# The FFN's down projection as seven half products in three slices, modulation rows made in the mixers, and Silu on ScalarE

## The chip, the cores and the metric

The kernel runs on one NeuronCore of a Trainium2 chip. The metric is the device time of one execution, in microseconds; lower is better. TensorE's time on a matmul is given by the profile in records: one fp32 matmul of the program leaves two MATMUL records and two LDWEIGHTS records, so 16 matmuls are 32 records.

## The reference, cut to what matters

Two blocks follow each other over 256 tokens of width 1024. The first has two layers. Each is `x + post_norm(mixer(pre_norm(x)))` and then `x + post_norm(swiglu(pre_norm(x)))`. Layer 0's mixer is a conformer convolution (31 taps) beside a gated linear recurrence, layer 1's an mLSTM. The feed-forward part, with 2816 hidden columns, is

```
def _swiglu(xn, w_gate, w_up, w_down):
    g = jnp.einsum('bsd,df->bsf', xn, w_gate)
    up = jnp.einsum('bsd,df->bsf', xn, w_up)
    return jnp.einsum('bsf,fd->bsd', jax.nn.silu(g) * up, w_down)
```

The second block (attention with spatial gating, a short convolution, and two mixtures of 32 experts) takes its shifts, scales and gates from "modulations": `silu(c) @ w_ada[l] + b_ada[l]` for both of its layers, 6144 columns each, and the first 2048 columns of layer 0 for `c_ctx` too. They depend on no token, so the kernel makes them during the first block, when DMA and VectorE have room.

## The kernel before, in words

Everything is fp32 and transposed: activations lie as tiles of 128 features (partitions) by 256 tokens. `h` is the FFN's input (8 tiles), `ff` its hidden activation (22 tiles), `u` and `sq` are other 8-tile buffers (`h`, `u`, `sq` and `ff` print as hsq and work in the profile).

**The weight stream.** SyncE (SP) loads weights in a fixed order, `chunks`, each up to 2 MB (128 partitions by 8 x 512 values), into `ring`, 6 slots used in turn. `load(n)` first waits until chunk n-6 is released by its reader, so SP stands still there with all that is behind it in the order. All these transfers are in SP's one queue. The list is: 0 to 3 input weights of mixer 0, 4 the first output half, 5 a slot without a transfer (convolution taps), 6 the second output half, then FFN 0, the mLSTM's six input and two output chunks, FFN 1, and the second block. `spread_groups` (L1736, DMA issues at L1741) copies activations between partitions with 16 small transfers, once for the recurrence's convolution and once for the 31-tap one. The second time stands ahead of `load(6)`.

**Mixer 0.** TensorE multiplies chunks 0 to 3 (L656, L568), does small products of the recurrence (L695), and then, when the second spread has landed, the 31-tap convolution (L670, 256 records), then layer norm sums and the output projection (L713, L585, L727).

**FFN, gate and up.** Hidden columns are done in chunks c = 0 to 5 of 512 (the last 256). c = 0 is a seam (`seam_chunk`, L638): it starts on the first 128 tokens while the norm of the others is still made. c = 5 is done plainly (L568, 128x256). c = 1 to 4, `quarter_products` (L785), use the Strassen-Winograd scheme on 2x2 blocks (tokens halved, columns halved, features halved): seven products P1, P5, P6, P2, P7, P3, P4 in place of eight, each 16 matmuls of 128 columns for gate and up together. VectorE makes the sums of weights (L2400, L2408, L2417, L2427, 128x1024) and tokens (L2383); ScalarE copies partial results between PSUM banks ("seeded"), VectorE adds the product P5 into two banks (L2444). Then ScalarE takes a Sigmoid of the gates and VectorE does two multiplications, gate by sigmoid (L2431) and that by up (L2432), three times a chunk.

**FFN, down.** Two column halves (c = 0, 1), each with 22 tiles of `ff` as contraction and four output tiles: 176 matmuls of 256 columns a layer (L870). In layer 0 the last output tile is done in token halves (22 + 22 matmuls of 128 columns, L870 and L898), so that the norm of the first tokens can be made under the second half.

**Modulations.** VectorE makes a row of 512 modulation values from one chunk of `w_ada` as one L2368 and seven L2215 instructions (`ada_make`), in half rows set between the FFN's other steps (`ada_steps`): 28 rows, since four chunks serve two conditions. TensorE collects four rows at a time (`ada_group`, L595, 8 records) in bank 7, four groups in layer 0 and three in layer 1, and turns each layer's result once (`ada_turned`, L607).

**Constants.** Two transfers (`spare_front`, `spare_back`, L1757 and L1758) reload constants over the FFN's weight sums, once the last quarter product is done, ahead of the next chunks.

Of the kernel before, what the change touches and what calls it, by code (L numbers as in the profile page):

```python
# [69 lines left out]
QW = HTL * CH // 2  # L70
ADA_LOADS = ((), (0, 1), (2,), (3, 4), (5,), (6,))
ADA_IN_DOWN = 7
ADA_ORDER = ((4, 5, 6, 7, 8, 9, 10, 11, 0, 1, 2, 3), tuple(range(12)))
# [75 lines left out]
def build(nc, a, out):  # L149
    with ExitStack() as ctx:  # L150
# [107 lines left out]
        fifth = tmp[:].rearrange("p a t -> p (a t)")  # L258

# [112 lines left out]
        down_part = sem("down_part_done")  # L372
# [26 lines left out]
        chunk(None)  # L399
        chunk(a["ab_w_out"][1])  # L400

        gate_chunks, up_chunks, down_chunks, ada_chunks = ([[], []] for i in range(4))

        def ffn_chunks(l):

            def ada_chunk(i):
                ada_chunks[l].append(len(chunks))
                chunk(a["w_ada"][l, ADA_ORDER[l][i]])

# [8 lines left out]
            for c in range(2):  # L418
                for k0 in range(0, FT, KT):
                    nk = min(KT, FT - k0)  # L420
                    down_chunks[l].append(len(chunks))
                    chunk(a["w_ff_down"][l, c, :, k0:k0 + nk, :], nk=nk)
                    if len(ada_chunks[l]) < 12:
                        ada_chunk(len(ada_chunks[l]))

        ffn_chunks(0)
        ffn_last = len(chunks) - 1
        for c in (0, 1, 2, 3, 4, 5):
            chunk(a["ml_w_in"][c])
        for c in range(2):  # L430
            chunk(a["ml_w_out"][c])
# [20 lines left out]
        seam_rows = (HTL + 2 * HTL, KT - 1 + 2, KT - 3 + 2 * 3)  # L452
        final_squares = 6 * KT + sum(seam_rows)
# [36 lines left out]
        def conditions(l, i):  # L490

            return 2 if l == 0 and i >= 8 else 1

        ADA_GROUPS = (4, 3)
        ADA_COPIES = (3, 1)
# [15 lines left out]
        def _(pe):  # L511
# [3 lines left out]
            made_so_far = [0]  # L515
# [24 lines left out]
            def next_chunk(n=None):  # L540
                if n is None:
                    n = state["chunk"]
# [45 lines left out]
            def ada_group(l, i):  # L588

                turn.take(S["ada_made"], GROUPS)  # L590
                if i == 0:
                    open_bank(7)
                last_group = i == ADA_GROUPS[l] - 1
                for g in range(GROUPS):
                    last = mm(ps[QUAD * g:QUAD * g + QUAD, 7, :], one_hot(i, QUAD), made[:, (GROUPS * i + g) % MADE, :],  # L595
                              start=(i == 0), stop=last_group, skip_group_check=True)
                if last_group:
                    close_bank(7, last, tiles_act, S["ada_rows"])
                else:
                    turn.give(last, S["ada_summed"])  # L600

            def ada_turned(l):
# [5 lines left out]
                close_bank(b, last, tiles_act, S["ada_raw"], reads=ADA_COPIES[l])  # L608
# [18 lines left out]
            def seam_chunk(n, w):  # L627

                banks = [next_bank() for m in range(4)]
                for t in range(TT):  # L630
                    for k in range(KT):
                        if k == 2:
# [83 lines left out]
            def halves_project():  # L716

                (first, w_0), (second, w_1) = next_chunk(), next_chunk(TAPS_SLOT + 1)
# [50 lines left out]
            def quarter_products(l, c):  # L769

                n = 4 * l + c - FAST.start
# [5 lines left out]
                def add(b, tile_of, rows, begins, first_sum=None):  # L777

                    for w in range(2):
                        if first_sum is not None:  # L780
                            pe.wait_ge(S["weights_summed"], 8 * n + first_sum + w)
# [32 lines left out]
                pe.wait_ge(S["tokens_summed"], 4 * l + 4)  # L814
                add(6, summed(0), sum_tokens[:, 0], True, 1)
                pe.wait_ge(S["seeded"], 4 * n + 1)
                add(1, summed(1), sum_tokens[:, 1], False, 5)
                add(0, plain(HTL, 0), high[:, :, half(0)], False)
                pe.wait_ge(S["seeded"], 4 * n + 3)
                pe.wait_ge(S["weights_summed"], 8 * n + 4)  # L820
                add(2, plain(0, 2), sum_tokens[:, 2], False)
                add(1, summed(2), high[:, :, half(1)], False, 7)
                pe.wait_ge(S["seeded"], 4 * n + 4)
# [2311 lines left out]
```

## Time and profile before

| | |
|---|---|
| median of three runs | 1881.2 us (1881.18 to 1881.66) |
| the profiled execution | 1880.99 us, its span 1879.2 us |
| TensorE busy | 1821.9 us, 97% |
| VectorE busy | 657.0 us, 35% |
| ScalarE busy | 376.0 us, 20% |
| mean DMA rate | 317 GB/s |
| FFN 0: c = 1 to 4, c = 5, down | 147 to 249, 249 to 263, 263 to 343 us |
| FFN 1: c = 1 to 4, c = 5, down | 516 to 622, 622 to 636, 636 to 715 us |
| the two stages of experts | about 860 to 1300 and 1460 to 1879 us |

In a line of the timeline the first number is the start, the second the time until the group's end, and "x64" how many records it joins; what stands in brackets is the engine's idle time before it and what ended that. Times on ScalarE and VectorE are ends of single instructions; matmuls overlap, so that 64 records of 380 ns take 13.8 us together. An instruction waits for the last of what it needs, and a full TensorE says only that it had work, not that the work was short.

### The profile page before, as it was taken

Reading aid. Unit: us, or ns where it says so; the run is one execution under the profiler, and the core shown is the slowest. Engines: PE = TensorE matmul, PEld = TensorE weight load, DVE = VectorE, ACT = ScalarE, POOL = GpSimd, SP = SyncE. Lnnn points to the kernel's source line nnn. Section 1 sums busy time; section 2 is a strip of 40 time slices with the busy share of each in tenths; the row PEclk is TensorE's granted clock in tenths of the full one; section 3 lists DMA queues with packets and bytes.
Section 4 is the critical chain, followed back from the end, with each engine's and each line's share of the span. In section 5 each row is a group of like instructions: output and inputs, shape, how many; then the busy total and the mean of one; then the engine's idle time right before and its main releaser. Section 6 shows DMA issues by size and latency. Waiting matters only on the chain.

```text
span 1879.2 us, 24366 instructions
## 1 busy us (share of the span) xinstructions
PE 1821.9 (97%) x10194; PEld 1200.2 (64%) x10196; DVE 657.0 (35%) x1353; ACT 376.0 (20%) x831; POOL 15.4 (1%) x31
## 2 busy tenths in 40 slices
PE   8999999999999999999999998999999999998998
PEld 7799988857999888575444433335885444433333
DVE  3278876432678653533111110112233111110112
ACT  3441110322311103423211110112013211111111
POOL 1000000000000100000000000000000000000000
PEclk9999999999999999999999999999999999999999
DMA  9744686732356883349999999999568999999996
GB/s 301 241 179 171 272 336 286 293 121 90 135 234 258 336 327 141 129 177 343 427 426 423 434 429 432 434 425 425 225 235 308 420 427 423 432 433 430 432 427 265
DMA packets 54323, 595.81 MB, mean 317 GB/s; under 512 B 6096, under 2 KB 20688, under 8 KB 24656
## 3 DMA queue, kind: packets, MB, share of 16 engines
q1 hardware_dynamic: 53648, 592.29, 76.9%
q10 hardware_dynamic: 576, 2.10, 0.3%
q8 instruction: 75, 1.23, 0.3%
q14 instruction: 24, 0.20, 0.0%
HBM read 588.90 MB, written 1.05 MB: 314 GB/s over the span
## 4 chain that ended last, share of the span: by engine, by line
PE 77%; DMA 19%; DVE 3%; ACT 1%; issue 0%; SPq 0%; DVEq 0%; ACTq 0%
PE ps L1357 18%; DMA ring<-in_w_up 17%; PE ps L568 16%; PE ps L870 8%; PE ps L785 7%; PE ps L1487 7%; PE ps L1312 3%; DMA ring<-in_w_ff_up 2%; PE ps L1305 2%; PE ps L638 2%; PE ps L924 1%; PE ps L727 1%; PE ps L656 1%; PE ps L670 1%; PE ps L1126 1%; PE ps L1086 1%
## 5 line engine op out<-in xcount | busy, mean ns | idle before, releaser
L1357 PE MATMUL ps<-ring,work 128*64 128x512 f32 x1792 | 405.8, 607 | 34.9 <-DMA ring<-in_w_up 29.6
L1357 PEld LDWEIGHTS ps<-ring,work 128*64 128x64 f32 x1792 | 128.8, 140 | 300.3 <-issue 248.2
L1804 ACT ACTIVATE work<-ps 128x512 f32<-128x512 f32 (+1 forms) x167 | 87.9, 532 | 696.2 <-PE ps L1487 248.7
L568 PE MATMUL ps<-hsq,ring 128*128 128x256 f32 x1024 | 225.1, 381 | 0.8 <-DVE hsq L2270 0.8
L568 PEld LDWEIGHTS ps<-hsq,ring 128*128 128x128 f32 x1024 | 193.9, 190 | 28.6 <-issue 2.8
L1487 PE MATMUL ps<-ring,work 128*64 128x512 f32 x864 | 191.6, 596 | 0.3
L2847 DVE TENSOR_TENSOR work<-ps,work 128x512 f32<-128x512 f32 x26 | 18.0, 691 | 389.2 <-ACT work L1804 389.2
L870 PE MATMUL ps<-work,ring 128*128 128x256 f32 (+1 forms) x704 | 149.5, 374 | 0.0
L2215 DVE SCALAR_TENSOR_TENSOR work<-ring,silu_c,work 128x512 f32<-128x512 f32 x196 | 143.7, 754 | 4.8
L870 PEld LDWEIGHTS ps<-work,ring 128*128 128x128 f32 x704 | 130.3, 190 | 20.7 <-issue 4.2
L1487 PEld LDWEIGHTS ps<-ring,work 128*64 128x64 f32 x864 | 59.6, 137 | 115.7 <-issue 113.9
L1312 PE MATMUL ps<-work 128*128 128x256 f32 x512 | 121.5, 382 | 0.0
L785 PE MATMUL ps<-hsq,ring 128*128 128x128 f32 x1024 | 118.1, 276 | 0.5 <-DVE work L2432 0.3
L785 PEld LDWEIGHTS ps<-hsq,ring 128*128 128x128 f32 x1024 | 116.2, 192 | 2.5 <-issue 2.2
L1312 PEld LDWEIGHTS ps<-work 128*128 128x128 f32 x512 | 92.7, 191 | 18.0 <-issue 8.1
L785 PE MATMUL ps<-hsq,spare 128*128 128x128 f32 x768 | 90.5, 279 | 2.0 <-ACT ps L1804 1.9
L785 PEld LDWEIGHTS ps<-hsq,spare 128*128 128x128 f32 x768 | 89.0, 195 | 2.7 <-ACT ps L1804 2.4
L2850 DVE TENSOR_TENSOR work<-ps,work 128x512 f32<-128x512 f32 x26 | 18.0, 691 | 195.0 <-PE ps L1357 195.0
L1804 ACT ACTIVATE work<-hsq 128x512 f32 x60 | 38.0, 634 | 209.8 <-PE ps L1357 202.5
L568 PE MATMUL ps<-work,ring 128*128 128x256 f32 x352 | 79.1, 382 | 0.4 <-DVE work L2687 0.4
L568 PEld LDWEIGHTS ps<-work,ring 128*128 128x128 f32 x352 | 66.2, 190 | 12.8 <-issue 3.5
L1357 PE MATMUL ps<-spare,work 128*64 128x512 f32 x192 | 56.2, 593 | 0.0
(347 smaller groups left out, 1617.9 us busy)
## 6 DMA issues: line engine op xcount, KB each, us to landing
ring<-in_w_up SPq DMA_DIRECT2D x16, 4096.0 KB, 22.0
ring<-in_w_down SPq DMA_DIRECT2D x16, 4096.0 KB, 20.4
ring<-in_w_gate SPq DMA_DIRECT2D x16, 4096.0 KB, 21.4
ring<-in_w_ada SPq DMA_DIRECT2D x24, 2048.0 KB, 11.1
ring<-in_w_gate SPq DMA_DIRECT2D x24, 2048.0 KB, 11.5
ring<-in_w_up SPq DMA_DIRECT2D x22, 2048.0 KB, 14.4
ring<-in_w_down SPq DMA_DIRECT2D x20, 2048.0 KB, 14.8
ring<-in_w_ff_gate SPq DMA_DIRECT2D x10, 2048.0 KB, 13.1
```

Of the source, the lines that this page charges most:

```text
L568: last = mm(ps[:, b, 0:T], w[:, k, m * P:(m + 1) * P], rhs[:, k, :], start=(i == 0), stop=(i == nk - 1))
L638: last = mm(ps[:, banks[m], half(t)], w[:, k, m * P:(m + 1) * P], u[:, k, half(t)], start=(k == 0), stop=(k == KT - 1))
L656: last = mm(ps[:, banks[m], 0:T], w[:, k, m * P:(m + 1) * P], u[:, k, :], start=(k == 0), stop=(k == KT - 1))
L670: last = mm(ps[QUAD * g:QUAD * g + QUAD, b, 0:T], taps_of(GROUPS * j + g), data_of(GROUPS * j + g), start=start, stop=stop)
L785: last = mm(ps[:, b, at:at + P], tile_of(w, k, m), rows[:, k, :], start=(begins and w == m == k == 0), stop=(k == HTL - 1), skip_group_che ...
L870: last = mm(ps[:, banks[m], 0:cols.stop], w[:, k - k0, m * P:(m + 1) * P], ff[:, k, cols], start=(k == 0), stop=(k == FT - 1))
L1305: last = mm(ps[:, 3 - half, k * PAIR:(k + 1) * PAIR], htok[:, t, (4 * half + k) * P:(4 * half + k + 1) * P], pick[:, t, :], start=(t == 0) ...
L1312: return mm(ps[:, 4 + m // 2, (m % 2) * T:(m % 2 + 1) * T], rows, first_spread if of_first else spread, start=begins and m % 2 == 0, stop= ...
L1357: last = mm(ps[e * CAP:(e + 1) * CAP, w, :], xg[:, k, e * CAP:(e + 1) * CAP], tile_of(first, w, i, 2 * k // KT, e, k % HTL), start=(k == 0 ...
L1487: last = mm(to, hg[:, at:at + CAP], tile, start=(k == 0), stop=(k == HTL - 1))
L1804: return nc.scalar.activation(out_, in_, f, bias=bias, scale=scale, **kw)
L2215: return V.scalar_tensor_tensor(out=out_, in0=in0, scalar=scalar, in1=in1, op0=op0, op1=op1)
```

## The change

1. **Down in seven products.** The 22 tiles of `ff` are split into tiles 0 to 10 and 11 to 21, the two operands of the 2x2 scheme's contraction; tokens and output columns are halved. The 11 tile pairs are taken in three slices of 4, 4 and 3 (`down_slice`). A slice has two chunks of weights (one for each column half) and seven products of 4 output tiles by 4 (or 3) contraction tiles, 128 columns each: 28 x 11 = 308 matmuls a layer. VectorE makes the sums of tokens (`down_tokens`, four a slice, 128x512) and of weights (`down_plus`, `down_second`, `down_less`, `down_fourth`, eight a slice, 128x1024) for each slice. The seven products add up in seven banks over the three slices. In the last slice VectorE joins the banks (`join_down`: four joins, three sums of 128x512) between the products, and one more matmul, identity by four tiles of `h`, adds the last term (P3's bank). ScalarE squares and copies four tiles at a time (`down_rows`) and VectorE sums four squares with one reduction (`sum_of_rows`). The norm of the first tokens starts under P5; `seam_chunk` after FFN 0 takes the other norm's sum two steps later (`late=4`).
2. **Modulation rows in the mixers.** Layer 0's first four `w_ada` chunks, which serve two conditions, become "pair" chunks: two loaded in mixer 0 (chunks 6 and 8, the second output half between them is 7), two in mixer 1 (after its second and fourth input chunk). VectorE makes their eight rows there in eight pieces of 8 instructions (`pair_part`; two pieces a chunk). The second `spread_groups` now stands behind `load(8)`. The other rows are 11 in FFN 0 (three of them of layer 1) and 9 in FFN 1. TensorE collects them in four groups a layer, the first of pair rows right after the seam, and FFN 1 has one more `ada_turned`.
3. **Gate function on ScalarE.** In c = 1 to 4 Silu replaces Sigmoid, and the multiplication L2431 goes: 24 instructions.
4. **Around it.** The constants' transfers wait for the last product of down, behind five chunks of the next stage; the waits for them on TensorE and VectorE move later. The context's squares go to other buffers, ahead of the sigmoids of c = 5.

```
@@ chunks
+        pair_chunk(PAIRS[0][0])
+        second_out = len(chunks)
         chunk(a["ab_w_out"][1])
+        pair_chunk(PAIRS[0][1])
+        ab_last = len(chunks) - 1
...
+            for s, n in enumerate(DOWN_SLICES):
+                two = {}
+                for c in (1, 0):
+                    two[c] = len(chunks)
+                    chunk(a["w_ff_down"][l, s, c, :, 0:2 * n, :], nk=2 * n)
+                down_chunks[l].append((two[0], two[1]))
+                for i in ADA_IN_DOWN[l][s]:
+                    ada_chunk(i)
@@ SP's order
-                if n == TAPS_SLOT + 1:
+                if n == ab_last + 1:
                     sp.wait_ge(S["lru_conv"], HTL)
                     spread_groups(rep_glu, cpad, REP, S["glu"], taps_spread)
...
+                load(n)
                 for l in range(2):
-                    if n == max(down_chunks[l]) + 1:
-                        sp.wait_ge(S["quarter_product"], 4 * QUARTERS * (l + 1))
+                    if n == max(down_chunks[l][-1]) + 6:
+                        sp.wait_ge(S["quarter_product"], UNITS * QUARTERS * (l + 1))
@@ TensorE, slices 0 and 1
+                    sums_by(4, 2)
+                    add("P6", summed(1), tokens[1])
+                    sums_by(6, 3)
+                    add("P7", plain(wb, 0), tokens[2])
+                    add("P5", summed(0), tokens[0])
+                    pe.wait_ge(S["tokens_summed"], tokens_by(l, s) + 4)
+                    add("P4", plain(wb, nk), tokens[3])
+                    release(nb, S["quarter_product"])
+                    add("P1", plain(wa, 0), low[:, :, half(0)])
+                    add("P2", plain(wa, nk), high[:, :, half(0)])
+                    pe.wait_ge(S["weights_summed"], 8 * u + 8)
+                    add("P3", summed(2), high[:, :, half(1)])
@@ TensorE, last slice: P1, P6, group, P7, (joined 1) P2, turned, (joined 2) P4, (3) P5, (4) P3
+                pe.wait_ge(S["proj_copied"], freed[S["proj_copied"]])
+                turn.give(mm(ps[:, DOWN_BANKS["P3"], :].rearrange("p (m t) -> p m t", m=4), ident, h[:, 4:KT, half(1)], start=False,
+                             stop=True, skip_group_check=True), S["quarter_product"])
@@ VectorE, mixers
+            pair_part(0, 0, 0)
+            pair_part(0, 0, 1)
             turn.take(S["lru_conv"], HTL)
             turn.take(S["lru_gate"], 2 * HTL)
             step(V.tensor_tensor(bx[:], bx[:], xr[:], ALU.mult))
+            pair_part(0, 1, 0)
...
                 step(V.tensor_tensor(cv[:, j, :], cv[:, j, :], tmp[:, 0, :], ALU.subtract), S["ln_ready"])
+            pair_part(0, 1, 1)
@@ VectorE, the gate in c = 1 to 4
-                step(V.tensor_tensor(sig, gates_, sig, ALU.mult))
-                step(V.tensor_tensor(rows, ups, sig, ALU.mult), S["quarter_read"])
+                step(V.tensor_tensor(rows, ups, silu, ALU.mult), S["quarter_read"])
@@ VectorE, down
                 last_quarter(n, c)
+                down_tokens(l, 0)
                 ada_steps(1)
+                down_plus(l, 0)
                 hidden(FAST.stop * HTL)
+                down_second(l, 0)
+                down_less(l, 0)
+                hidden(FAST.stop * HTL + 1)
                 ada_steps(1)
+                down_fourth(l, 0)
+                ada_steps(2)
+                down_tokens(l, 1)
...
```

## Rows read from the trace of the kernel before

**Rows 1.** The page, sections 1 and 2: busy time, and GB/s in 40 slices of 47 us.

```profile
PE 1821.9 (97%) x10194; PEld 1200.2 (64%) x10196; DVE 657.0 (35%) x1353; ACT 376.0 (20%) x831; POOL 15.4 (1%) x31
...
GB/s 301 241 179 171 272 336 286 293 121 90 135 234 258 336 327 141 129 177 343 427 426 423 434 429 432 434 425 425 225 235 308 420 427 423 432 433 430 432 427 265
```

**Rows 2.** What TensorE waited for: line and releaser, us in total, times, longest.

```profile
PE ps L1357 <- DMA ring<-in_w_up: 29.6, 15, 2.6
...
PE ps L785 <- ACT ps L1804: 1.9, 1, 1.9
```

**Rows 3.** Chain of waits, pieces: start us, us, line and records (128 columns L785, 256 L870).

```profile
151.06 21.45 PE ps L785 x192
...
223.89 25.21 PE ps L785 x224
...
635.91 13.81 PE ps L870 x64
```

**Rows 4.** Timeline, TensorE: down of FFN 0, and the seam after it.

```profile
262.75 13.98 PE L870 MATMUL ps<-work,ring 128*128 128x256 f32 x64
...
276.66 1.06 PE L595 MATMUL ps<-work,hot 128*32 128x512 f32 x8
...
343.30 1.95 PE L638 MATMUL ps<-work,ring 128*128 128x128 f32 x16
```

**Rows 5.** Timeline, TensorE: down of FFN 1 from its start to the next product.

```profile
635.74 1.46 PE L870 MATMUL ps<-work,ring 128*128 128x256 f32 x6
...
714.97 1.24 PE L568 MATMUL ps<-work,ring 128*128 128x256 f32 x5
```

**Rows 6.** Timeline of mixer 1: 16 records of 512 columns (for the identity matmul).

```profile
373.68 7.13 PE L924 MATMUL ps<-ring,hsq 128*128 128x512 f32 x16
```

**Rows 7.** VectorE by line and shape: xcount | busy us, mean ns | idle before.

```profile
L2400 DVE TENSOR_TENSOR spare<-ring 128x1024 f32<-128x1024 f32 x16 | 19.1, 1222 | 13.6 <-DMA ring<-in_w_ff_up 8.8 <-DMA ring<-in_w_ff_gate 4.7
...
L2383 DVE TENSOR_TENSOR hsq<-hsq 128x512 f32<-128x512 f32 x8 | 5.5, 691 | 0.3
...
L2645 DVE TENSOR_REDUCE small<-work 128x1 f32<-128x512 f32 x2 | 1.4, 686 | 2.4 <-ACT work L1804 2.3
```

**Rows 8.** Timeline, FFN 0: load at the end of c = 4, half rows in down.

```profile
249.13 0.33 SPq L1603 DMA_DIRECT2D ring<-in_w_ff_down  x1
...
282.23 9.36 DVE L2215 SCALAR_TENSOR_TENSOR work<-ring,silu_c,work 128x512 f32<-128x512 f32 x14
```

**Rows 9.** Timeline, FFN 1, c = 2 and 3, around TensorE's wait, and the clock of that window.

```profile
541.50 0.33 SPq L1603 DMA_DIRECT2D ring<-in_w_ada  x1
...
562.40 1.22 DVE L2400 TENSOR_TENSOR spare<-ring 128x1024 f32<-128x1024 f32 x1 [3.67 <-DMA ring<-in_w_ff_up]
...
573.98 0.69 DVE L2431 TENSOR_TENSOR work<-ps,work 128x512 f32<-128x512 f32 x1 [0.73 <-ACT work L1804]
...
576.13 5.47 PE L785 MATMUL ps<-hsq,spare 128*128 128x128 f32 x32 [1.91 <-ACT ps L1804]
...
575.00:580.00 5.00, 3.87 (x21) 3.88 (x22) 4.83 (x8) 1.08 (x2) 0.00 (x0) 0.69 0.99 423
```

**Rows 10.** Timeline, mixer 0: spreads and loads on SP, and where TensorE needs the second spread.

```profile
37.97 0.59 SPq L1603 DMA_DIRECT2D ring<-in_ab_w_out  x1
...
52.89 10.34 SPq L1741 DMA_DIRECT2D work<-work  x16
...
69.71 5.60 PE L670 MATMUL ps<-work,ring 128*32 128x256 f32 x100
```

**Rows 11.** DMA between 31 and 39 us, where spreads stood behind others: GB/s in 40 parts.

```profile
GB/s 184 287 128 205 143 149 230 246 169 174 184 246 190 184 200 184 190 266 190 195 189 179 215 236 205 200 230 220 200 205 215 210 210 195 195 205 179 220 200 205
```

**Rows 12.** VectorE's idle stretches in the mixers (in brackets), timeline.

```profile
66.97 1.23 DVE L2324 TENSOR_TENSOR work<-work 128x1024 f32<-128x1024 f32 x1 [15.90 <-ACT work L1804]
...
94.91 1.75 DVE L2219 RECIPROCAL rstd<-root 128x256 f32<-128x256 f32 x1 [6.87 <-ACT root L1804]
...
373.89 0.42 DVE L2550 COPY work<-ps 128x256 f32<-128x256 f32 x1 [11.66 <-PE ps L916]
```

More of the change, by code:

```diff
@@ L488, in build, with unit, slice_unit, product_done @@
         SPARE_DMAS = [sum(spare_dmas(i, half) for i, _ in matrices(RING // 2, TURNING - 1)) for half in range(2)]
[L490 to L495, printed above, removed]
+        ADA_COPIES = (4, 2)
+        PAIR_COPIES = 2
+        made_by = 0
+        for l in range(2):
+            for n in pair_chunks[2 * l:2 * l + 2]:
+                made_by += 2
+                released[n] = (S["ada_made"], made_by)
+            for n in ada_chunks[l]:
+                made_by += 1
+                released[n] = (S["ada_made"], made_by)
+        def unit(l, c):
+            return UNITS * l + c - FAST.start
+        def slice_unit(l, s):
+            return UNITS * l + len(FAST) + s
+        def product_done(u, name):
+            s = u % UNITS - len(FAST)
+            order = ORDERS["gate" if s < 0 else "last" if s == len(DOWN_SLICES) - 1 else "down"]
+            return QUARTERS * u + order.index(name) + 1
+        def seeds_before(l, c):
+            return (4 * len(FAST) + 1) * l + 4 * (c - FAST.start)
+        def joins_before(l, c):
+            return (len(FAST) + 4) * l + c - FAST.start
+        def tokens_by(l, s=-1):
+            return 4 * (len(DOWN_SLICES) + 1) * l + 4 * (s + 1)
         def masks_by(pair):
@@ L890, in ffn @@
-                state["chunk"] = max(down_chunks[l]) + 1
-                if l:
-                    return
-                open_bank(6)
-                for k in range(FT):
-                    if k == KT - 2:
-                        sum_stats(half(0))
-                    n, w = held[k // KT]
-                    last = mm(ps[:, 6, 0:P], w[:, k % KT, 3 * P:4 * P], ff[:, k, half(1)], start=(k == 0),
-                              stop=(k == FT - 1))
-                    if k % KT == KT - 1:
-                        turn.give(last, down_part)
-                        release(n, down_part)
@@ L2303, in _, with ada_part, pair_part, ada_make @@
             step(V.tensor_scalar(lamt[:, 16:20], lamt[:, 12:16], LRU_C / 2, None, ALU.mult), S["lam_ready"])
+            def ada_part(n, part, rows):
+                slot = ring[:, n % RING, :].rearrange("p (k c) -> p k c", k=KT)
+                if part == 0:
+                    dve.wait_ge(slot_loaded[n % RING], landed(n))
+                for k in range(part * KT // 2, (part + 1) * KT // 2):
+                    for w, to in enumerate(rows):
+                        by = silu_c[:, k, w:w + 1]
+                        if k:
+                            turn.own(vchain, len(rows) - 1 - (w if k == KT - 1 else 0))
+                            last = stt(to, slot[:, k, :], by, to, ALU.mult, ALU.add)
+                        else:
+                            last = V.tensor_scalar(to, slot[:, k, :], by, None, ALU.mult)
+                        turn.give(last, S["ada_made"] if k == KT - 1 else vchain)
+            def pair_part(l, i, part):
+                ada_part(pair_chunks[2 * l + i], part, pair_rows[2 * i:2 * i + 2])
+            def ada_make(l, q, part):
+                if part == 0 and q >= MADE and (q - MADE) % GROUPS == 0:
+                    turn.take(S["ada_summed"])
+                ada_part(ada_chunks[l][q], part, [made[:, q % MADE, :]])
             def make_taps(dst, w):
@@ new lines, in down_second @@
+            def down_second(l, s):
+                n, u = down_chunks[l][s][0], slice_unit(l, s)
+                dve.wait_ge(slot_loaded[n % RING], landed(n))
+                dve.wait_ge(S["quarter_product"], product_done(u - 1, "P6"))
+                for w in range(2):
+                    dve.wait_ge(S["weights_summed"], 8 * u + 1 + w)
+                    ((w11, _), _), sums = down_blocks(l, s, w)
+                    turn.give(V.tensor_tensor(sums[1], sums[0], w11, ALU.subtract), S["weights_summed"])
@@ L2515, in ffn @@
                         weights_fourth(l, c)
+                    elif l:
+                        turn.take(S["ada_raw"], PAIR_COPIES)
                     ada_steps(2)
```

501 lines of the change are left out of this document (330 added, 171 removed).

## The prediction

> **What bounds the kernel now.** I read the page first [rows 1]: TensorE is busy 97% of the span. Two stages differ in kind. From slice 19 of 40 on, with a break in the middle, DMA runs at 420 to 434 GB/s and TensorE's waits name expert weights [rows 2]; before that DMA moves 90 to 343 GB/s a slice, and TensorE hardly waits. The whole change lies in the first 16 slices, where TensorE's work is the time. What is won there moves the start of everything behind it, the loads of the experts too, since they wait for slots released by the stage before. So I sum TensorE's path through mixers and FFNs, and then look for waits that the change brings.
>
> The price of a record comes from the chain's long pieces [rows 3]: 128 columns take 21.45/192 = 0.1117 and 25.21/224 = 0.1125 us, 256 columns 13.81/64 = 0.2158. I take 0.1122.
>
> **Down, seven for eight.** FFN 0 before: 262.75 to 343.30, 80.55 us [rows 4]. Its parts: 308 wide records (66.5), 88 narrow (9.9), three groups of modulation rows at 276.66 to 277.65, so 1.0 each, and 1.1 of small things (the turn, a norm's sum, gaps). After: 616 narrow records, 69.1; the identity matmul, two records of 512 columns at 7.13/16 = 0.44 [rows 6], 0.9; two groups, 2.0; the same small things, 1.0. That is 73.0, so -7.6. FFN 1 before: 714.97 - 635.74 = 79.23 [rows 5], all 352 records wide. After: 73.1, so -6.1. The bounds of the rate move the two by -0.6 and +0.4 together.
>
> The row on this has a rule beside it that speaks against narrow products. The Trainium skill (TensorE: Matmul & The Clock Gate, section LDWEIGHTS) has a weight load cost its columns over 1.2, 107 ns for 128, however few columns the matmul then streams: going from 256 to 128 columns leaves no room behind the load. By that rule alone 616 loads would take 65.9 us where the row's price gives 69.1, so the load would just keep up; the row decides.
>
> **Modulation groups.** Each FFN has a pair group after the seam, +1.0 each, and FFN 1 one more turn, +0.4: +2.4. TensorE's work alone is then -7.6 - 6.1 + 2.4 = -11.3.
>
> **Can VectorE feed it?** 128x1024 sums are 1.22 us, 128x512 ones 0.69 [rows 7], a half row 9.36/14 x 4 = 2.7 [rows 8]. In FFN 0 between 249.6 and slice 2's start: tokens 3 x 4 x 0.7 = 8, weights 24 x about 1.1 = 26, ten half rows 27, hidden tiles 2: 63 us of about 65. I walked it in order: slice 0 starts at 262.8 and a product takes 32 x 0.1122 = 3.6, so slice 1 starts at 289 and its first sums are done at 283; slice 2 starts at 314, P6 needs its sums at 317, they are done at 310. The joins: P7 ends at 323, two additions of 0.7, P4 starts after P2 and the turn at 326. Each is covered by a product in front. FFN 1 has 10 us more (context norm) and fewer rows; slack 6 at slice 1. Cost 0, by the 6 us of slack; without it see the third case.
>
> **Start of down.** Slice 0 needs both its chunks where down needed one. Their slots come free when c = 4 ends (the load at 249.13 [rows 8]). Two times 2.1 MB at 430 GB/s is 9.8 us: 259.3 at the soonest. In rows 9 three loads and a 1 MB one (7.3 MB, 17.1 us by rate) issued from 541.5 were there at 562.4, 3.8 us more; so 259.3 to 263.1. `down_second` adds 2.4 after that, and TensorE is there at 262.7: a wait of 0 to 2.9 a layer. I take 0.35 each, near the low end since only two chunks are in the queue: +0.7.
>
> **Silu.** VectorE loses 24 multiplications, off the path in FFN 0. In FFN 1 they are on it: the load at 562.4 sets off sums, two gate steps, ScalarE's copy, and TensorE waits 1.9 us until 576.13 [rows 9]. Its next 32 records take 5.47 where the piece before took 3.6 to 3.7, and the granted clock of 575 to 580 is 0.69: part at 1.2 GHz after that idle time, 1.7 us lost. Leaving out 0.42 and 0.69, plus issue gaps, gives -1.2, and a wait of about 1.1 stays. Bounds: 0, and -2.9 if after the shorter wait the clock stays at 2.4 GHz. I take -1.2. ScalarE's table loads for Silu fall where it idles for products.
>
> **Ends of down.** FFN 0: the first tokens' norm starts under P5, about 3.7 us ahead of the seam, before 2.9; the second norm's sum is taken two steps later and is ready. Cost 0; 0 to 1. FFN 1: after P3 a 128x512 square and a 128x512 reduction (0.69 [rows 7]) and an addition stand where a 128x256 square and addition stood; the sum then comes 0.3 later than TensorE's place for it: +0.4, 0 to 0.8. The constants now come after two output chunks: 4.2 + 2.7 MB from 6.5 us before down's end, there at about 12 us after it, needed at 16. Cost 0.
>
> **Mixers, VectorE.** A `pair_part` is 8 instructions, 5.4 us. In mixer 0 two go into the 15.9 us of idle before 66.97, one into the 9.4 behind, one into the 6.9 before 94.91; in mixer 1 two (10.8) into the 11.7 before 373.89 [rows 12], the others between heads. The tightest has 0.9 to spare. Cost 0.
>
> **Mixer 0, the queue.** Here is what the change costs. SP's order was: load 4 at 37.97, then wait for the recurrence's convolution and issue the 16 spreads from 52.89 to 62.6, TensorE needing them at 69.71 [rows 10]. Now loads 6, 7 and 8 are ahead of the spreads: 6 and 7 right after 4 (their slots are long free), 8 when chunk 2 is released, at about 50.4. Spreads move slowly: with a backlog (31 to 39 us) DMA gives 180 to 230 GB/s, mostly near 205 [rows 11]. Chunk 4 ended near 47.3. Then 6 and 7: +9.8, 57.1; 8: +4.9, 62.0; 16 spreads of 142 KB, 2.27 MB at 205: +11.1, 73.1, and 0.4 for the last to land: 73.5 against 69.7. TensorE waits 3.8. After it the clock: the only row with such a wait lost 1.7 [rows 9], so +5.5 in all. Bounds: 0 if the spreads are not held back, 8.4 with 184 GB/s (+1.2) and twice the clock's loss.
>
> The Trainium skill (DMA: Bandwidth & Descriptors, Queues, rings and completion order) says that each DMA engine consumes a queue's descriptors in ring order. By that rule the spreads stand behind all three loads and the 5.5 holds; without it the sum is the second case's.
>
> **Sum.** -11.3 - 1.2 + 0.7 + 0.4 + 5.5 = -5.9. The profiled execution took 1880.99, 1.8 more than its span; the median of the runs is 0.2 above it. From 1881.2: 1875.3.
>
> **The cases.**
> 1. *As summed*, 1875.3, by its own bounds 1872 to 1878.5. Chance 0.5.
> 2. *The spreads are in time* (the loads of pair chunks share the engines with them, or the rate in a mixed queue is higher): -5.5 more, 1869.8; 1866.5 to 1872. For it: in the middle of 37 to 47 us, loads and spreads went together. Against: that stretch was as long as the two one after the other. Chance 0.26.
> 3. *VectorE or the loads hold down back at the slice borders.* VectorE has 63 us of work in 65, and each chunk's slot waits for the product or row that uses it. Once it is over 6 us late, each layer's slices 1 and 2 wait for sums; with 3 us a layer and its clock loss the result is 1881 (1878 to 1885). For it: rows 9 show one late load running through to TensorE. Against: my walk. Chance 0.16.
> 4. *Slower: the narrow products in down are slower than in gate and up.* The place is both downs, where TensorE reads `ff`, sums and ring while VectorE writes sums and DMA fills slots at over 400 GB/s. 1232 records: it decides from 9.7/1232 = 7.9 ns a record more, 0.120 us; at 0.122 the result is 1887. Against it stands 0.1125 over 224 records under the same kinds of load [rows 3]. Chance 0.08.
>
> **Numbers.** No change to a measurement of this kernel is within 0.2%, 1877.4 to 1885.0. Faster: 0.44 of case 1, case 2, a little of 3: 0.71. Within: 0.06 of case 1 and most of 3: 0.2. Slower: 0.09. The range must hold 8 in 10: 1867 to 1880 holds cases 1 and 2 and the lower part of 3.
>
> **What the profile after would show.** Down as 616 records a layer in about 69 us and next to no wait in front of its products; 8 groups and 3 turns; no L2431; the context's squares ahead of FFN 1's down. In mixer 0 SP issues three loads between the two spreads, and the 31-tap convolution starts near 73.5 with a wait of 3 to 5 us on DMA and a lower clock right behind it; from there to the FFN everything is later by 5. In FFN 1 the wait in c = 3 is near 1.1. The experts' part keeps its length. I am wrong if the convolution starts before 71 (then case 2), if down's waits sum to over 4 us (case 3), or if 32 of its records take over 3.8 us (case 4).

## The result, and the profile after

The changed kernel takes 1892.64 us, median of five runs (1888.59 to 1894.71), against 1881.66 before: a ratio of 1.0057, 95% interval 1.0044 to 1.0070. It is slower by 0.57%. The forecast was 1875.3 with a range of 1867 to 1880, and the chance of slower was given as 0.09, for a cause (slow narrow records) that did not occur. The profiled execution took 1894.71, its span 1892.8 against 1879.2.

The page's first section, and what TensorE waited for in the changed kernel (line and releaser, us in total, times, longest):

```profile
PE 1813.4 (96%) x10688; PEld 1202.6 (64%) x10688; DVE 725.7 (38%) x1412; ACT 382.2 (20%) x824; POOL 17.4 (1%) x31
```

```profile
PE ps L1469 <- DMA ring<-in_w_up: 30.5, 16, 2.6
PE ps L734 <- issue: 14.7, 1, 14.7
...
PE ps L1469 <- issue: 4.5, 1, 4.5
...
PE ps L920 <- DVE spare L2659: 3.1, 2, 1.8
```

TensorE is busy 8.5 us less than in [rows 1], so the seven products for eight do save work, and the span is 13.6 us longer. The waits for expert weights are as in [rows 2] (L1357 is now L1469). New are one wait of 14.7 us at the 31-tap convolution (L734, before L670), two in front of down (L920), and 4.5 us inside the experts' second stage.

I set the starts of the same stages beside each other in both traces. What each stretch added to the lead of the old kernel, in us:

| stretch | added |
|---|---|
| start of the 31-tap convolution (69.71, now 84.31) | +14.6 |
| convolution to FFN 0's seam (half clock) | +2.05 |
| seams and pair groups, both FFNs | +1.8 |
| c = 1 to 4: FFN 0, FFN 1 | -0.4, -2.8 |
| c = 5 and the start of down, both | +3.9 |
| down FFN 0; down FFN 1 with all up to the experts | -7.3, -5.5 |
| seam behind FFN 0 | +1.1 |
| experts, first stage and the mixer behind | +0.1 |
| experts, second stage | +5.9 |
| sum | +13.5 |

Everything outside mixer 0 and the experts' second stage adds up to -9.1. The two others cost 22.6. The start of down in FFN 0 and the seam behind it, 73.24 us apart in the changed kernel, read:

```profile
281.65 3.81 PE L920 MATMUL ps<-hsq,spare 128*128 128x128 f32 x32 [1.78 <-DVE spare L2659]
...
354.89 3.73 PE L702 MATMUL ps<-work,ring 128*128 128x128 f32 x32
```

**Mixer 0.** The timeline of the changed kernel, TensorE and then SP's issues (start, time until the group's end), and what the spreads' line shows over both times 16 transfers (min/median/max, in ns and then in us):

```profile
84.31 16.07 PE L734 MATMUL ps<-work,ring 128*32 128x256 f32 x256 [14.65 <-issue]
```

```profile
50.36 0.33 SPq L1715 DMA_DIRECT2D ring<-in_w_ada  x1
52.76 19.29 SPq L1853 DMA_DIRECT2D work<-work  x16
72.09 1.17 SPq L1715 DMA_DIRECT2D ring<-in_w_ff_gate  x1
```

```profile
L1853 SPq DMA_DIRECT2D work<-work x32: 601/608/7774, 26.6 to 71.4; - x32
...
DMA to landing us min/median/max: 6.9/8.0/15.4
```

In [rows 10] the 16 issues took 10.34 us; now they take 19.29, for one of them, the ninth, took 7.77 (58.73 to 66.5). The first went out at 52.76 and landed at 67.0; the last went out at 71.4 and landed 12.8 us later, at 84.2; TensorE starts at 84.31. The profile calls the wait "issue", for it finds no releaser, but time and place name the spreads. The rate between 30 and 100 us, in 40 parts of 1.75 us, shows the loads at over 400 GB/s until 63 and the spreads near 200 behind them:

```profile
GB/s 320 112 164 200 211 206 225 209 235 422 431 403 431 412 431 412 440 449 409 209 122 163 206 207 207 205 225 191 200 377 361 161 53 20 0 0 0 9 0 0
```

The next windows give busy time, granted clock, DMA share and rate of two stretches:

```profile
64.00:78.00 14.00, 5.66 (x27) 4.63 (x25) 10.78 (x17) 9.54 (x16) 0.00 (x0) 0.89 1.08 189
78.00:84.00 6.00, 0.00 (x0) 0.00 (x0) 5.51 (x7) 1.65 (x2) 0.00 (x0) 0.50 0.95 288
```

From 64 to 84 us DMA moved 14 x 189 + 6 x 288 = 4.4 MB, and the 16 spreads are 2.27 MB. The rest is weights: the end of chunk 8, for which VectorE waited until 72.15, and FFN 0's first gate chunk, issued behind the spreads and under way with the last of them. TensorE's granted clock is 0.50 before it resumes, and the 256 records of the convolution then take 16.07 us where they took 14.02 before: the 2.05 us of the table.

**The experts' second stage.** The product of the second up matrix in the changed kernel:

```profile
1441.39 0.64 PE L1469 MATMUL ps<-ring,work 128*64 128x512 f32 x1
1446.51 8.78 PE L1469 MATMUL ps<-ring,work 128*64 128x512 f32 x31 [4.48 <-issue]
```

In the kernel before the same 32 records stand in one piece of 7.09 us from 1433.76 on. A matmul leaves two records, so this gap falls inside one. The profile names no releaser, and the program (`product_of`) has no wait at this place: it waits only ahead of the first and of the ninth matmul of this product.

### The profile page after: what moved, and what is told of

Same layout as the page of the kernel before. It is cut to its first block, busy times and chain, and to the rows that moved or that the text cites. A ratio compares the mean times of both kernels' runs of the same rounds, so it can differ in the third digit from the quotient of the medians.

```text
span 1892.8 us, 25468 instructions
## 1 busy us (share of the span) xinstructions
PE 1813.4 (96%) x10688; PEld 1202.6 (64%) x10688; DVE 725.7 (38%) x1412; ACT 382.2 (20%) x824; POOL 17.4 (1%) x31
## 4 chain that ended last, share of the span: by engine, by line
PE 75%; DMA 18%; DVE 4%; issue 2%; ACT 1%; SPq 0%; DVEq 0%; ACTq 0%
PE ps L1469 18%; DMA ring<-in_w_up 17%; PE ps L627 14%; PE ps L850 9%; PE ps L920 7%; PE ps L1599 7%; PE ps L1424 3%; PE ps L1417 2%; PE ps L1036 1%; PE ps L702 1%; PE ps L791 1%; DMA ring<-in_w_ff_up 1%; PE ps L734 1%; PE ps L720 1%; PE ps L1238 1%
## 5 line engine op out<-in xcount | busy, mean ns | idle before, releaser
L1469 PE MATMUL ps<-ring,work 128*64 128x512 f32 x1792 | 407.7, 608 | 39.2 <-DMA ring<-in_w_up 30.5
L1469 PEld LDWEIGHTS ps<-ring,work 128*64 128x64 f32 x1792 | 129.2, 140 | 306.0 <-issue 254.5
L2371 DVE SCALAR_TENSOR_TENSOR work<-ring,silu_c,work 128x512 f32<-128x512 f32 x140 | 105.9, 756 | 4.8
L627 PEld LDWEIGHTS ps<-work,ring 128*128 128x128 f32 x352 | 66.1, 190 | 13.8 <-issue 3.9
L1469 PE MATMUL ps<-spare,work 128*64 128x512 f32 x192 | 56.2, 592 | 0.0
L1916 ACT ACT_TABLE_LOAD x39 | 50.0, 1283 | 20.9 <-PE ps L1469 11.1
L702 PE MATMUL ps<-work,ring 128*128 128x128 f32 x384 | 45.6, 276 | 1.5 <-ACT work L1916 1.5
## 6 DMA issues: line engine op xcount, KB each, us to landing
ring<-in_w_gate SPq DMA_DIRECT2D x24, 2048.0 KB, 11.1
ring<-in_w_down SPq DMA_DIRECT2D x20, 2048.0 KB, 14.7
```

The lines of the kernel that those rows point to most:

```text
L627: last = mm(ps[:, b, 0:T], w[:, k, m * P:(m + 1) * P], rhs[:, k, :], start=(i == 0), stop=(i == nk - 1))
L702: last = mm(ps[:, banks[m], half(t)], w[:, k, m * P:(m + 1) * P], u[:, k, half(t)], start=(k == 0), stop=(k == KT - 1))
L1469: last = mm(ps[e * CAP:(e + 1) * CAP, w, :], xg[:, k, e * CAP:(e + 1) * CAP], tile_of(first, w, i, 2 * k // KT, e, k % HTL), start=(k == 0 ...
L1916: return nc.scalar.activation(out_, in_, f, bias=bias, scale=scale, **kw)
L2371: return V.scalar_tensor_tensor(out=out_, in0=in0, scalar=scalar, in1=in1, op0=op0, op1=op1)
```

## The experiments

Each is compared with the kernel before, timed anew beside it (medians of 1882.25 us for experiments 1 to 4, 1882.67 for 5 to 8, 1882.4 for 9 to 11). Each profile shows one execution. Three groups: the queue in mixer 0, the gap in the second stage, and the parts that behaved.

**1. One load ahead of the second spread.**

```
-                if n == ab_last + 1:
+                if n == TAPS_SLOT + 2:
                     sp.wait_ge(S["lru_conv"], HTL)
```

> The changed kernel with one edit: in SP's order the second spread stands behind one weight load (the first pair chunk, 6) and no longer behind three (6, 7 and 8). In the changed kernel the 31-tap convolution started at 84.31 us after 14.65 us of idle TensorE. Theory S (the loads ahead of the spreads in the one queue make the wait): chunk 6 landed at 58.0 where three loads shared the way; with only chunk 4 and 6 ahead the engines are through with them near 55, the 16 spreads are issued from 52.8 and 2.27 MB at about 205 GB/s end near 66 to 68, before TensorE is there at 69.7. The convolution starts near 69.7 without a wait, everything behind it is 14.6 + 2.1 (the half clock after the idle time) = 16.7 us earlier: 1892.6 - 16.7 = 1875.9 us, 1874 to 1880 with the spread of the runs. Chunk 8 would land near 73, as it did at 72.15. Rival (the second output half and the pair chunk, now late, stop VectorE's recurrence or the output projection): the wait comes back ahead of the recurrence's mix or the projection, 1880 to 1888.

1885.64 us, ratio 1.0019 (1.0009 to 1.0029). The convolution starts at 69.68, without a wait: the theory's step is right. But the rival is right too. Two lines of this kernel, VectorE's and TensorE's:

```profile
78.74 0.88 DVE L2501 TENSOR_SCALAR spare<-ring,silu_c 128x512 f32<-128x512 f32 x2 [10.24 <-DMA ring<-in_w_ada]
```

```profile
89.93 9.48 PE L791 MATMUL ps<-work,ring 128*128 128x256 f32 x32 [4.31 <-issue]
```

VectorE stands 10.24 us for the second pair chunk, and the recurrence's scan and the layer norm's start, next in its program, with it; the projection waits 4.31. The seam comes at 123.3 (before 116.46, changed 133.1).

**2. Two loads ahead** (`TAPS_SLOT + 3`).

> The changed kernel with the second spread behind two loads (6 and 7; both can be issued at once, their slots are free) and ahead of chunk 8. Theory S with the forecast's own rates (each load 4.9 us of queue at 430 GB/s, then 11.1 us for the spreads): 4.9 us less backlog than in the changed kernel, so the convolution starts at about 84.3 - 4.9 = 79.4, minus 2 us for chunk 8 that no longer shares the way: 77 to 80, total 1884 to 1888. If instead the jump comes from SP itself (one of its 16 issues took 7.8 us with three loads under way, as if the queue were full), two loads leave the queue room, no issue takes over 2 us, and the spreads land by 66 to 70: convolution at 69.7, total about 1876.

1890.1 us (1.0045; 1.0029 to 1.0060), above the 1884 to 1888 that was expected. Convolution at 76.91 after 7.24 us, and no issue of SP was long (16 in 11.61 us, the longest 1.54). The spreads are late all the same; SP's long issue is not needed for a wait.

**3. Three loads ahead, in the kernel before.**

```
-                if n == TAPS_SLOT + 1:
+                if n == TAPS_SLOT + 4:
                     sp.wait_ge(S["lru_conv"], HTL)
...
-                if n == 8:
+                if n == TAPS_SLOT + 5:
                     sp.dma_start(rw[:], a["router_w"]).then_inc(consts_loaded, 16)
```

> The kernel before, with nothing changed but SP's order: the second spread (and the router's weights behind it) stands behind three loads of 2 MB, here the second output half and FFN 0's first gate and up chunks (chunks 6, 7 and 8 of its own list, the third of which waits for the release of input chunk 2, as in the changed kernel). No pair rows, no half products in down. Theory S: the 31-tap convolution starts near 84 us where it started at 69.71, at half clock for its first part, and the total is 1881.7 + 16.7 = 1898.4 us, 1895 to 1901. Rival (the wait needs the rest of the change, VectorE's pair rows ahead of the recurrence above all): the convolution starts before 76 and the total is 1881 to 1889.

1893.25 us (1.0070; 1.0054 to 1.0085): this one edit makes the kernel before as slow as the changed one. In its profile the wait is 6.84 us, convolution at 77.67: less than 14.65, and between the numbers of theory and rival. FFN 0's seam is 9.4 us later than before; most of the other 3.5 of the 13.0 by which the span grew lies in the experts' part, whose code this edit leaves alone. So mixer 0 accounts for 9.4 us here, not for 16.65 as in the changed kernel, and the likeness of the totals is no measure of it.

**4. One load, and P1 and P2 first in slice 0.**

```
+                        add("P1", plain(wa, 0), low[:, :, half(0)])
+                        add("P2", plain(wa, nk), high[:, :, half(0)])
                     sums_by(4, 2)
...
+                    if s:
                         add("P1", plain(wa, 0), low[:, :, half(0)])
                         add("P2", plain(wa, nk), high[:, :, half(0)])
```

> The first kernel of this set (one load ahead of the spread), and in each layer's down TensorE takes slice 0's products in the order P1, P2, P6, P7, P5, P4, P3 in place of P6, P7, P5, P4, P1, P2, P3. P1 and P2 need one chunk as loaded and no sums of weights. In the changed kernel down started with a wait of 1.78 us (FFN 0) and 1.35 us (FFN 1) on VectorE's second sum, behind a chunk that landed 12.8 us after its issue. Theory: the chunk itself is there before TensorE (278.9 against 279.9), so both waits go: 3.1 us less than the first kernel of this set, with up to 0.5 us of half clock on top. Rival (the chunk's slot is released two products later, the next loads are late, and the same wait stands in front of slice 1 or 2): within 1 us of the first kernel.

1887.13 us (1.0027): no gain, the rival is right. In front of down there is no wait in either layer, but 1.16 us (FFN 0) and 1.50 (FFN 1) stand in front of slice 1: by the stages 1.9 and 1.5 us were won at the start of down and 2.0 and 1.8 lost behind it. Here the convolution waited 2.17 us with one load ahead.

**5. Dead code ahead of the jump, changed kernel.** The experts' stages begin with a branch on how many tokens an expert has; the code for all tokens is skipped.

```
+                if first == moe_first[1]:
+                    for _ in range(12):
+                        mm(ps[:, 7, T:2 * T], zeros[:, 0:P], zeros[:], start=False, stop=False, skip_group_check=True)
```

> The changed kernel with 12 matmuls more in the branch of TensorE's program that is not taken (all tokens for every expert) ahead of the second experts' stage; nothing that runs is changed, only where the code behind the jump lies, 48 instructions further. In the changed kernel and in all three kernels made from it so far TensorE stood 3.2 to 4.5 us in that stage after the first record of a matmul, where no wait on a semaphore can stand, with half clock behind it; the stage took 431.1 to 432.1 us where it took 425.7 and 426.1 in the two kernels with the old code. Theory C (the jump's target lies just ahead of the end of a block of code, and the next block is fetched only after the jump; the fetches show as 16384-byte packets of the instruction queue, 256 instructions of 64 bytes): the target now lies at the start of the next block, the gap is gone, the stage takes 426, and the total is 1892.6 - 6 = 1886.6 us (1885 to 1888.5). Rival (the gap is a late load or DMA traffic of instructions as such, which the small shift doesn't touch): gap still there, 1891 to 1894.

The gap is gone, and the second stage (from the product behind the gathering of tokens to the last group of L1469) takes 425.8 us where it took 431.6. The total is 1889.38 (1883.29 to 1895.94), above the 1885 to 1888.5 expected; in the profiled run the wait in mixer 0 was 17.09 us.

**6. Dead code, kernel before** (the same lines, 58 in place of 12).

> The kernel before with 58 matmuls (232 instructions) more in the same branch that is not taken, ahead of its second experts' stage. Counted in the two programs, the changed kernel's code in front of that jump is 1007 instructions longer, which is 17 less than four blocks of 256, and so puts the target 17 instructions lower in its block; 232 more put the target of the kernel before 24 lower. Theory C: the same standstill appears in a kernel that has nothing of the change, 3 to 5 us within a few matmuls behind the jump, the stage takes 430 to 432.5 and the total is 1882.2 + 6 = 1888 us (1886 to 1889.5). Rival (not the position of the code): 1881.5 to 1883, no gap.

1887.62 us (1.0026; 1.0017 to 1.0035), the second stage 432.8 (425.7 in the kernel before). The gap stands where it was foretold, in a kernel that has nothing of the change:

```profile
1433.25 1.08 PE L1357 MATMUL ps<-ring,work 128*64 128x512 f32 x4
1438.61 8.50 PE L1357 MATMUL ps<-ring,work 128*64 128x512 f32 x28 [4.28 <-issue]
```

The windows 1436 to 1438 and 1438 to 1444 of this kernel show what follows: a granted clock of 0.60 and 0.56.

```profile
1436.00:1438.00 2.00, 0.00 (x0) 0.00 (x0) 1.88 (x8) 0.00 (x0) 0.00 (x0) 0.60 0.90 367
1438.00:1444.00 6.00, 5.39 (x16) 2.29 (x17) 0.00 (x0) 0.00 (x0) 0.00 (x0) 0.56 0.48 205
```

Two more readings of the traces bear on the cause. The DMA view has this row of the instruction queue (packets, MB, share) for 1444.0 to 1445.2 in the changed kernel, and the second for 1436.4 to 1437.5 in this one:

```profile
q8 instruction: 1, 0.02, 5.2%
...
q8 instruction: 1, 0.02, 5.4%
```

So one packet of 16 KB moves 1.2 to 1.5 us before TensorE goes on (1446.51 and 1438.61), and none does in the 5 us from 1438.5 and from 1431. And the place of the gap moves with the code: the jump stands ahead of the last four of the 32 records of the gate product, so the gap comes 7 records behind its target in the changed kernel (4, 2 and 1) and 10 in this one (4, 2 and 4). Three records and their weight loads are 6 instructions, where the two targets, 17 and 24 instructions lower, lie 7 apart.

**7. Mixer 0 put in order.** Experiment 1 with the 12 dead matmuls, and:

```
-            pair_part(0, 1, 0)
             turn.take(S["lru_powers"], HTL)
...
-            pair_part(0, 1, 1)
+            pair_part(0, 1, 0)
             inverse_root()
...
                 step(V.tensor_tensor(y_conf[:, j, :], cv[:, j, :], sgate[:, j, :], ALU.mult), S["mixed"])
+            pair_part(0, 1, 1)
```

> The kernel with one load ahead of the second spread, plus two edits. First, VectorE takes the third and fourth piece of the pair rows (the second pair chunk, which then landed at 78.7 us) after the layer norm's subtractions and after the gated product, in place of ahead of the recurrence's scan; there VectorE had stood 10.24 us for the chunk, and TensorE 4.31 us in front of the output projection. Second, the 12 dead matmuls of the run above. Theory: the projection starts without a wait, FFN 0's seam near 116.5 (it was 123.3), and the standstill in the experts' second stage is gone: 1885.6 - 6.8 - 6 = 1872.8 us, 1871 to 1875. Rival for the mixer (the fourth piece, now at about 102 to 107.5, holds back the sums of squares ahead of FFN 0's norm): seam at 118 to 120, 1875 to 1877.

1875.6 us, ratio 0.9965 (0.9951 to 0.9979), 0.6 above the range that was expected. Convolution at 69.70, seam at 116.45, to 0.01 us where they were before.

**8. And P1 alone first in slice 0.**

```
+                        add("P1", plain(wa, 0), low[:, :, half(0)])
                     sums_by(4, 2)
...
+                    if s:
                         add("P1", plain(wa, 0), low[:, :, half(0)])
```

> The kernel just described, and in slice 0 of each down the product P1 (one chunk as loaded, no sums) ahead of P6; the rest keeps its order. With P1 and P2 both ahead the wait of 1.8 and 1.4 us in front of down went, and one of 1.2 and 1.5 us came in front of slice 1, since P4, whose token sums VectorE overwrites for slice 1, ended 7.2 us later. With P1 alone ahead it ends 3.6 us later, and VectorE's sums for slice 1 are then due at about 663.9 against 666.8 in FFN 1: no wait at either place. Theory: 3.1 us less than the kernel just described, 1869.7 us. Rival (VectorE is full in this stretch, and what is taken from one wait comes back at the next): within 0.8 us of it.

1869.57 us (1868.67 to 1870.03), ratio 0.9932 (0.9919 to 0.9946). It beats both kernels. Its starts of down, FFN 0 and FFN 1, and slice 0 behind each:

```profile
263.95 3.73 PE L920 MATMUL ps<-work,ring 128*128 128x128 f32 x32
267.52 3.74 PE L920 MATMUL ps<-hsq,spare 128*128 128x128 f32 x32
...
629.78 3.73 PE L920 MATMUL ps<-work,ring 128*128 128x128 f32 x32
633.35 3.74 PE L920 MATMUL ps<-hsq,spare 128*128 128x128 f32 x32
```

No idle time stands in brackets. Its convolution started at 70.60, without a wait. By the stages this edit gave 1.7 and 1.5 us; the rest of the 6.0 between the two medians lies in the experts' part, which differs by such amounts between profiles. That the total came out at the 1869.7 foretold is therefore luck: the start was 2.8 us above the 1872.8 assumed, and the step 2.9 us larger.

**9. Silu alone, kernel before** (three `ACT.Sigmoid` to `ACT.Silu`, L2431 left out).

> The kernel before with the third part of the change alone: Silu on ScalarE in place of Sigmoid in c = 1 to 4, and the multiplication of the gate by its sigmoid (24 instructions on VectorE) left out. The forecast gave it -1.2 us, with a bound of -2.9 if TensorE's clock holds behind the shorter wait; in the changed kernel c = 1 to 4 of FFN 1 took 103.3 us where they took 106.1, and FFN 0's 101.7 where they took 102.0. If Silu is the cause: 103.3 to 103.8 in FFN 1, the wait in c = 3 at 1.1 to 1.2 us without half clock behind it, total 1882.5 - 3 = 1879.5 us. If the cause lies elsewhere (the moved modulation rows, the order of the loads): 105 to 106, total 1881.3 to 1882.5.

1878.8 us, ratio 0.9982 (0.9973 to 0.9992). FFN 1's c = 1 to 4 take 103.2 us, FFN 0's 101.7. The wait in c = 3 and the clock around it:

```profile
574.27 3.84 PE L785 MATMUL ps<-hsq,spare 128*128 128x128 f32 x32 [1.19 <-ACT ps L1804]
```

```profile
573.00:578.00 5.00, 3.81 (x34) 3.73 (x34) 4.86 (x7) 1.11 (x3) 0.00 (x0) 1.00 1.03 439
```

**10 and 11. What makes 14.65 out of 6.84?** Experiment 5 with all of VectorE's pair pieces behind the convolution; and experiment 5 with mixer 0's pair chunks read from the projection's weights (its modulations are then other numbers).

> The changed kernel with the 12 dead matmuls, and all four pieces of the pair rows on VectorE behind the 31-tap convolution (the first after the layer norm's subtractions, three after the gated product); SP's order is the changed kernel's, three loads ahead of the second spread. The wait in front of the convolution was 14.65 and 17.1 us with VectorE at the pieces from 58 us on, and only 6.8 us in the kernel before with three loads and an idle VectorE. If VectorE's reads and writes slow the spreads: a wait of 6 to 9 us. If they don't: 12 to 17 us as in the changed kernel. The pieces behind the gated product delay FFN 0's first norm by some 8 us in either case, so the wait in front of the convolution is what counts, not the total: about 1889 + 8 less the gain.

> The changed kernel with the 12 dead matmuls, and the two pair chunks of mixer 0 loaded from the output projection's weights in place of the modulation's (same shape and size; the pair rows are then other numbers): everything else, SP's three loads ahead of the spread too, as in the changed kernel. If the source of the modulation chunks makes the queue slower than the kernel before with three loads was (6.8 us of wait against 14.65 and 17.1): a wait of 6 to 9 us and a total near 1883. If not: 12 to 17 us, 1888 to 1891.

The waits were 9.92 and 8.90 us. The second lies where the source's theory has it, but the first, with the old source, is just as short and lies between the numbers of its own theory; neither cause is shown. The first took 1892.51 us; the total of the second (2864.7) says nothing, since with other modulations the router's numbers send the kernel down the branch for all tokens.

## Why the prediction was wrong

**The step that failed: "Mixer 0, the queue".** The sentence "2.27 MB at 205: +11.1, 73.1, and 0.4 for the last to land" took the spreads as a block that begins when the loads end and then has the queue alone. The first half held roughly: the rate fell from over 400 to about 200 GB/s at 63 (forecast 62.0), though the last of chunk 8 came only at 72. The second didn't. The spreads needed 21 us from there, not 11.1. Two things fall into that time: SP got eight of them out by 58.7 and the other seven behind the long one only after 66.5, and the last ones shared the engines with the load issued behind them. How much each of the two took, no run separates. So the wait was 14.65, not 3.8, and the loss to the clock 2.05, not 1.7: 16.65 against 5.5, outside the bounds of 0 to 8.4. The bounds varied the rate and the clock's loss and left the two other things at nothing.

The Trainium skill's rule that each DMA engine consumes a queue's descriptors in ring order (DMA: Bandwidth & Descriptors, Queues, rings and completion order) gave the right side against case 2. The traces agree in so far as no spread landed before 67 us. They also show that transfers of one queue don't land in the order of their issue: chunk 8, issued ahead of all the spreads, landed at 72.1, five us behind the first of them, and by the 4.4 MB weights issued behind the spreads moved before the last spread was complete.

That the backlog makes the wait is shown: it is 0, 2.2, 0 and 0 us with one load ahead (experiments 1, 4, 7, 8), 7.2 with two, and 6.8, 8.9, 9.9, 14.7 and 17.1 with three. A second load is dearer than the first, and a third may cost nothing or 10 us. What chooses within 6.8 to 17.1 is open. Experiment 5's ten runs spread over 12.7 us, experiment 1's ten over 8.2 and experiment 8's five over 1.4, so part of it may differ from run to run in one kernel, which one profile of each can't show; VectorE's rows and the source of the chunks were tried once each and not settled. SP's longest single issue goes along with it: 1.5 and 2.1 us at waits of 7.2 and 6.8, 4.0 and 3.9 at 8.9 and 9.9, 7.8 at 14.7, 10.7 at 17.1. Which of the two is the cause isn't shown.

**A term the forecast didn't have: where the code lies.** "The experts' part keeps its length" was wrong by 5.9 us. The instruction queue (packets, MB, share of 16 engines) has this row in the changed kernel:

```profile
q8 instruction: 79, 1.29, 0.3%
```

These are 16 KB each, and before there were 75; TensorE's code in front of the jump was 1007 instructions shorter, counted in the two programs. Moving the target of a jump that is always taken by 48 instructions took the gap away, and by 232 in the old kernel made it. The Trainium skill (Runtime: NRT & Kernel Launch, Instruction fetch mechanics) has a taken branch stop the sequential prefetch. The traces agree in that the gap stands behind a taken jump, and add that the cost depends on the target's place in its block: none in the kernel before, and in the changed kernel and experiment 6, where the gap comes 7 and 10 records behind the target, 4.5 and 4.3 us and then half clock, together 5.9 and 7.2 for the stage. That the code's position sets the gap is shown both ways. That the gap is the fetch of the next block is argued, from the packet of 16 KB shortly before its end and from the place that moves with the code; why this packet comes no sooner stays open.

**By the forecast's other terms.**
- Down FFN 0, forecast -7.6: 73.24 us against 73.0, so -7.3. Its 32 narrow records take 3.74 us less the overlap, 3.57 from start to start (experiment 8's rows show the same), 0.112 each. Case 4 is refuted, and the concern that a narrow matmul leaves no room for its weight load shows no cost here: 0.112 is half of the 0.2158 of 256 columns.
- Down FFN 1 to its end, -6.1 and +0.4: -6.7, +0.8 for the tail and +0.5 behind it, -5.5 in all.
- Modulation groups, +2.4: +1.8.
- Silu, -1.2: -2.8 in FFN 1 and -0.4 in FFN 0. The mechanism was right and the bound was the value. The wait fell to 1.18, as forecast, and the clock held: 1.00 (584 to 589 us) where [rows 9] have 0.69. Experiment 9 has it alone: -2.8 and -0.4 too.
- Start of down, +0.7: +3.9. I took "near the low end". In FFN 0 chunk one landed 7.2 us and two 12.8 us after the issue, in the bounds of 10.2 to 14; VectorE then needs 2.4. In FFN 1 the chunks were there, and VectorE was late: two of its four 128x512 sums took 1.10 and 1.22 us in place of 0.69, and the instructions behind them were slow too. GpSimd was at work on the context's norm at that very time; in FFN 0, where it was idle, all four took 0.69, with DMA at 401 GB/s there and 406 in FFN 1. Experiments 7 and 8 show the same 1.10 and 1.22 beside GpSimd. So GpSimd is the likely cause, though no run tries it alone. The wait is 1.78 and 1.35, and 0.15 to 0.6 more lie in the stretch.

```profile
634.86 0.69 DVE L2630 TENSOR_TENSOR hsq<-work,hsq 128x512 f32<-128x512 f32 x1
635.58 1.10 DVE L2630 TENSOR_TENSOR hsq<-work 128x512 f32<-128x512 f32 x1
...
635.00 1.14 POOL L1896 TENSOR_TENSOR tmp<-tmp,spare 128x256 f32<-128x256 f32 x1 [616.50 <-ACT spare L1916]
```

- VectorE at the slice borders, 0: right. Between slices no wait stands, until experiment 4 moved P4 and used up the slack.
- Ends of down, 0 in FFN 0: +1.1, the second half's norm is late by 0.85.
- VectorE's pieces in the mixers, 0: right for time, but they depended on chunk 8, and experiment 1 shows the price as soon as it is late.

Without the queue and the code the forecast's terms give -11.4 and the traces -9.1. Experiment 8, which removes both, and the waits of down, measures -13.1; in its profile 11.5 of that are there when the experts begin.

## What to carry to other kernels

Small transfers that TensorE waits for do not belong behind weight loads in one queue: one 2 MB load ahead cost 0 to 2 us here, two 7, three 7 to 17. When they are moved forward, look at who waits for the load that is now late, and reorder that engine too. And when a stage that nobody changed gets slower, look for a gap without a releaser behind a jump: dead code in front of the target tests it without changing what runs.

## What the hardware showed that was not expected

- One DMA issue on SP took 7.77 us where the others took 0.6, with three loads of 2 MB and eight spreads issued shortly before.
- 48 instructions that never run were worth 5.8 us in a stage of 430 us; 232 in another kernel cost 7.2.
- Behind a wait of 1.91 us TensorE's next 32 records took 5.47 us [rows 9]; behind waits of 1.18, 1.35 and 1.78 us they took 3.84, 3.81 and 3.81.
- Two 128x512 sums of VectorE took 1.10 and 1.22 us while GpSimd was at work, in three kernels; the same sums in FFN 0, with GpSimd idle, took 0.69.
